# Head and group sums of squares of a mixer block: one fp32 pass over the squares, or two fp32r passes over their high and low part

## The chip, the cores and the metric

The kernel runs on one core of a Trainium2 chip. Its time is the device time of one execution, in microseconds (us). The engines are TensorE (PE in the profile, its weight loads PEld), VectorE (DVE), ScalarE (ACT), GpSimd (POOL) and SyncE (SP), which issues nearly all loads.

## The reference

Two transformer blocks run one after the other on 512 tokens of width 1024. The change is in the mixer of the first one:

```python
    z = u @ w_in
    c0 = 3 * CONV_WIDTH
    cb, cc, ch = jnp.split(z[..., :c0], 3, axis=-1)
    rq, rk, rv, rg = jnp.split(z[..., c0:], 4, axis=-1)
    y_conv = cb * causal_dwconv3(cc * ch, conv_w)
    y_conv = group_rms_norm(y_conv, conv_norm_g, CONV_GROUPS)
    ...
    o = chunkwise_retention(q, k, v).reshape(b, s, RET_WIDTH)
    y_ret = group_rms_norm(o, ret_norm_g, RET_HEADS) * jax.nn.silu(rg)
    return jnp.concatenate([y_conv, y_ret], axis=-1) @ w_out
```

`group_rms_norm` divides each value by the root of the mean square of its group: 128 channels for each of the 4 retention heads, 64 for each of the 8 convolution groups.

## The kernel before

Everything is held with channels on the 128 partitions and the 512 tokens along the row, so a sum over a group of channels is a sum over partitions. TensorE makes it by multiplying the squares with a matrix of ones (`ones`, one head of 128) or with a block matrix (`group64`, two groups of 64).

Every product with a weight is three fp32r matmuls: the weight tile `raw` is split by ScalarE into `w_hi` (L893) and by GpSimd into `w_lo` = raw - w_hi (L443), the activations are split in the same way (`u_hi`, `u_lo`, later `y_hi`, `y_lo`), and a *unit* (L480) adds w_hi·u_hi, w_hi·u_lo and w_lo·u_hi over 8 chunks: 24 matmuls. Weight tiles go through 4 slots. The sums of squares, the retention scores and the transposes are plain fp32 matmuls.

Each engine runs its own list of instructions in the order in which the code is written; semaphores tie the lists together. The stage around the change comes right after the first norm, at about 46 to 232 us.

- **Retention, 4 heads.** A loop pass j of TensorE is `ret(j, j-1)`: unit 0 (v) of head j, the scores of head j-1 (`ret_scores`, L551), unit 1 (q), the output of head j-1 (`ret_out`, L558, which releases the semaphore `ret_o`), the transposes of v, unit 2 (k), then `ret_sum` (L564), and unit 3 (the gate). The sum of head 3 comes in the convolution's opening, behind that stage's first unit 2. The third score matmul of a head waits until VectorE has multiplied the first with its decay (`sdec`, L1384).
- ScalarE copies the head's output (`osb`, L989), squares it (`nsq`, L990), and takes the root of the sum (`ret_root`, L993).
- VectorE turns v into `vf` (`v_in`, L1353), makes `sdec`, rotates q and k (`rotate`, L1371 to L1376), inverts the root (L1389), applies gain and gate, makes `y_lo` (L1400) and the gate of the next head (`silus`, L1412).
- **Convolution, 4 pairs of groups.** A loop pass j of TensorE is units 0 and 1 of pair j, `conv_sum(j-1)` (L615), unit 2 of pair j. The sum of the last pair stands inside the first output units (`two_units(st_out, ...)`). VectorE makes the product (`conv_in`, L1432 and L1436), the three taps and two more multiplications (`conv`, L1443 to L1454, which ends in `ycv_done`), ScalarE squares it (`csq`, L1027), TensorE sums it, ScalarE takes the root (`conv_root`, L1030), VectorE inverts it (L1458) and normalizes.
- ScalarE splits weight tiles between these steps (`ahead`); the first two splits for the output projection stand behind the last `conv_root`.

Of the kernel before, what the change touches and what calls it, by code (L numbers as in the profile page):

```python
# [25 lines left out]
F32R = mybir.dt.float32r  # L26
# [4 lines left out]
P = 128  # L31
T = 512
# [108 lines left out]
def wait(eng, sem, n):  # L141

    if not isinstance(n, int) or n > 0:
        eng.wait_ge(sem, n)
# [23 lines left out]
def build(nc, tab, x, norm1_g, w_in, conv_w, conv_norm_g, ret_norm_g, w_out, norm2_g, w_up, w_down,  # L168
# [23 lines left out]
    with ctx:  # L192
        def sb(name, shape, dt=F32, where=ctx):
            return where.enter_context(nc.sbuf_tensor(name, shape, dt))
# [3 lines left out]
        def sem(name):  # L198
            if name not in sems:
                sems[name] = ctx.enter_context(nc.semaphore(name))  # L200
            return sems[name]
# [32 lines left out]
        start = ExitStack()  # L234
        xtok = sb("xtok", [P, NT, D], where=start)
        start.close()
        acc = sb("acc", [P, 6 * D], where=one)
        mix = ExitStack()
        rope = sb("rope", [P, 2, T], where=mix)
# [226 lines left out]
        def _(pe):  # L466
# [93 lines left out]
                last.then_inc(sem("ret_o"), 1)  # L560

            def ret_sum(p):
                pe.wait_ge(sem("osq_ready"), p + 1)
                pe.matmul(ps[:, SA, :], ones[:], nsq[:, 0, :], start=True, stop=True).then_inc(sem("ret_sum"), 1)  # L564

            def ret(j, p):
                unit(st_ret, 0, j, u_hi, u_lo)
# [43 lines left out]


            def conv_sum(p):
                pe.wait_ge(sem("csq_ready"), p + 1)
                pe.matmul(ps[:, SB, :], group64, nsq[:, 1, :], start=True, stop=True  # L615
                          ).then_inc(sem("conv_sum"), 1)

            unit(st_conv, 0, 0, u_hi, u_lo)
            ret_scores(NQ - 1)
# [265 lines left out]
        def _(act):  # L885
# [101 lines left out]
            def osq(p):  # L987
                act.wait_ge(sem("ret_o"), p + 1)
                act.activation(osb[:], ps[:, OU, :], ACT.Copy).then_inc(sem("osb_ready"), 1)  # L989
                act.activation(nsq[:, 0, :], ps[:, OU, :], ACT.Square).then_inc(sem("osq_ready"), 1)  # L990
            def ret_root(p):
                act.wait_ge(sem("ret_sum"), p + 1)
                act.activation(nrs[:], ps[:, SA, :], ACT.Sqrt, bias=epsc[:, 0:1], scale=1.0 / P  # L993
                               ).then_inc(sem("ret_root"), 1)
# [29 lines left out]
            def csq(j):  # L1024
                act.wait_ge(sem("ycv_done"), j + 1)
                wait(act, sem("conv_sum"), j)
                act.activation(nsq[:, 1, :], ycv[:], ACT.Square).then_inc(sem("csq_ready"), 1)  # L1027
            def conv_root(p):
                act.wait_ge(sem("conv_sum"), p + 1)
                act.activation(sg[:], ps[:, SB, :], ACT.Sqrt, bias=epsc[:, 0:1], scale=1.0 / HD  # L1030
                               ).then_inc(sem("conv_root"), 1)
# [223 lines left out]
        def _(dve):  # L1255
# [110 lines left out]
            def rotate(s, j, dst):  # L1366

                dve.wait_ge(used[s], st_ret.turn(s, j) + 1)
                h = P // 2
                dve.wait_ge(sem("rotated"), 2 * j + s - 1) if not (isinstance(j, int) and 2 * j + s - 1 <= 0) else None  # L1370
                dve.tensor_tensor(nt[0:h, 2, :], ps[h:P, s, :], sinr[h:P, :], ALU.mult).then_inc(sem("swapped"), 1)  # L1371
                dve.tensor_tensor(nt[h:P, 2, :], ps[0:h, s, :], sinr[0:h, :], ALU.mult).then_inc(sem("swapped"), 1)
                dve.tensor_tensor(dst[:], ps[:, s, :], cosr, ALU.mult).then_inc(bank_free[s], 1)
                dve.wait_ge(sem("swapped"), 4 * j + 2 * s)
                dve.wait_ge(bank_free[s], st_ret.turn(s, j) + 1)
                dve.tensor_tensor(dst[:], dst[:], nt[:, 2, :], ALU.add).then_inc(sem("rotated"), 1)  # L1376
                dve.wait_ge(sem("rotated"), 2 * j + s)
                dve.sem_inc(sem("qk_ready"), 1)

            def ret_decay(p):  # L1380
                for b in range(NT):
# [2 lines left out]
                    dve.tensor_tensor(sdec[:, b:b + 1, 0:n], ps[:, SA + b % 2:SA + b % 2 + 1, 0:n],  # L1384
                                      decay[:, ds(p, 1), 0:n], ALU.mult).then_inc(sem("sdec_ready"), 1)

            def ret_norm(p):
                dve.wait_ge(sem("ret_root"), p + 1)
                dve.reciprocal(nrs[:], nrs[:]).then_inc(sem("ret_rinv"), 1)  # L1389
                dve.wait_ge(sem("ret_rinv"), p + 1)  # L1390
                dve.wait_ge(sem("osb_ready"), p + 1)
                dve.scalar_tensor_tensor(nt[:, 0, :], osb[:], vec[:, ds(VAT["ret_norm_g"] + p, 1)], nrs[:],
                                         ALU.mult, ALU.mult).then_inc(sem("ret_t"), 1)
                dve.wait_ge(sem("ret_t"), p + 1)
                dve.wait_ge(sem("silu_ready"), p + 1)
                dve.tensor_tensor(nt[:, 1, :], nt[:, 0, :], silu[:], ALU.mult).then_inc(sem("ret_y"), 1)
# [13 lines left out]
            def silus(j):  # L1410
                dve.wait_ge(sem("sg_ready"), j + 1)
                dve.tensor_tensor(silu[:], silu[:], sg[:], ALU.mult).then_inc(sem("silu_ready"), 1)  # L1412
# [2 lines left out]
            rotate(2, 0, kf)  # L1415
            gate_in(0)
            silus(0)
            with dve.Fori(1, NQ) as j:
                v_in(j)
                ret_decay(j - 1)  # L1420
                rotate(1, j, qf)
                rotate(2, j, kf)
                ret_norm(j - 1)
                gate_in(j)
                ret_lo(j - 1)
                silus(j)


            def conv_in(j):
                dve.wait_ge(used[0], st_conv.turn(0, j) + 1)  # L1430
                wait(dve, sem("prod_ready"), j)
                dve.tensor_tensor(ccs[:], ps[:, 0, :], r1sq[:], ALU.mult).then_inc(bank_free[0], 1)  # L1432
                dve.wait_ge(used[1], st_conv.turn(1, j) + 1)
                dve.wait_ge(bank_free[0], st_conv.turn(0, j) + 1)
                wait(dve, sem("conv_y3"), j)
                dve.tensor_tensor(prod[:, 2:T + 2], ps[:, 1, :], ccs[:], ALU.mult).then_inc(sem("prod_ready"), 1)  # L1436
                dve.wait_ge(sem("prod_ready"), j + 1)
                dve.sem_inc(bank_free[1], 1)
# [26 lines left out]

            ret_decay(NQ - 1)
            dve.wait_ge(sem("vf_turned"), NQ)
            dve.tensor_tensor(r1sq[:], r1[:], r1[:], ALU.mult).then_inc(sem("r1sq"), 1)
            dve.wait_ge(sem("r1sq"), 1)
            conv_in(0)  # L1470
            ret_norm(NQ - 1)
            ret_lo(NQ - 1)
            dve.wait_ge(sem("masks"), 2)
            conv(0)
            with dve.Fori(1, NQ) as j:
                conv_in(j)
                conv_norm(j - 1)
                conv(j)
            conv_norm(NQ - 1)
            dve.wait_ge(sem("ycv_ready"), NQ)  # L1480
            dve.sem_inc(sem("mix_done"), 1)
# [52 lines left out]
            def mlp(st, name, scale, with_ada, next_norm, factor=None):  # L1534
# [63 lines left out]
                for i in range(2):  # L1598
# [1 line left out]

            dve.wait_ge(sem("brow_out"), 16 * NQ)
            dve.tensor_tensor(gsq[:], vec[:, VAT["final_norm_g"]:VAT["final_norm_g"] + KC],
                              vec[:, VAT["final_norm_g"]:VAT["final_norm_g"] + KC], ALU.mult).then_inc(sem("gsq"), 1)
            dve.wait_ge(sem("gsq"), 1)
            dve.tensor_scalar(gones[:], ones[:], gsq[:, KC - 1:KC], None, ALU.mult).then_inc(sem("gones"), 1)
            mlp(st_mlp, "mlp", None, True, "n3", factor=nrs)
            dve.wait_ge(sem("gains"), 2)
# [188 lines left out]
```

## Time and profile before

| | |
|---|---|
| three runs | 1453.22, 1456.02, 1457.69 us, median 1456.02 |
| the profiled execution | 1455.06 us, of which the traced span is 1453.2 us |
| TensorE busy | 1416.0 us, 97% of the span |
| VectorE, ScalarE, GpSimd busy | 794.0, 491.5, 567.8 us |
| mean granted TensorE clock | 0.983 |
| fp32 sums of squares touched by the change | 8, of 2 matmul records each, 0.59 us a record |

An fp32 matmul of 512 columns shows as two records. Records of TensorE overlap, so what one costs is read from the distance between starts and not from its length. The number in brackets at the end of a row is the time in which the engine had nothing to do before it, and who ended that.

### The profile page before, as it was taken

The numbers are of one execution on the slowest core, as the hardware profiler recorded it, in microseconds if no ns is written. First come the engines' busy times: TensorE is split into PE (matmuls) and PEld (weight loads), VectorE is DVE, ScalarE is ACT, GpSimd is POOL, SyncE is SP. The second block draws the span as 40 slices with busy tenths as digits, with TensorE's granted clock in tenths as the row PEclk, the third lists the DMA queues.
The fourth block names the chain that finished last, engine by engine and source line by source line (L and its number), as shares of the span: only waits on it lengthen the run. The fifth ranks groups of instructions, "written<-read, shape, count | busy, mean of one in ns | idle before, by whom it ended". The sixth has DMA issues, their size and how long they took to land.

```text
span 1453.2 us, 18921 instructions
## 1 busy us (share of the span) xinstructions
PE 1416.0 (97%) x6382; PEld 1116.0 (77%) x6382; DVE 794.0 (55%) x1094; ACT 491.5 (34%) x717; POOL 567.8 (39%) x230
## 2 busy tenths in 40 slices
PE   7999999999999999999999999999989999999998
PEld 6677777888787888876667666788868888888886
DVE  6655666485766757876998444311235535253343
ACT  4332324332323223235433333332335323142243
POOL 3433334363454544422212211344343635445441
PEclk9999999999999999979999999999999999999998
DMA  7643234464664746434112121233332423324231
GB/s 200 134 91 91 72 87 145 116 180 124 184 189 133 202 123 180 110 109 139 53 49 57 45 58 44 73 89 103 98 101 72 117 76 113 98 80 121 74 87 58
DMA packets 244644, 155.40 MB, mean 107 GB/s; under 512 B 7764, under 2 KB 237520, under 8 KB 244344
## 3 DMA queue, kind: packets, MB, share of 16 engines
q1 hardware_dynamic: 244136, 153.56, 37.7%
q10 hardware_dynamic: 464, 1.27, 0.3%
q8 instruction: 25, 0.41, 0.1%
q14 instruction: 19, 0.16, 0.0%
HBM read 150.08 MB, written 4.73 MB: 107 GB/s over the span
## 4 chain that ended last, share of the span: by engine, by line
PE 51%; DVE 2%; ACT 1%; issue 0%; DVEq 0%; ACTq 0%
PE ps L480 41%; PE ps L824 3%; PE ps L732 3%; PE ps L758 1%; PE ps L749 1%; PE ps L736 1%; DVE prob L1685 0%; DVE work L1712 0%; PE ps L719 0%; PE ps L543 0%; PE ps L738 0%; DVE top L1710 0%; DVE nt L1648 0%; DVE prob L1677 0%; DVE otok L1772 0%
## 5 line engine op out<-in xcount | busy, mean ns | idle before, releaser
L443 POOL TENSOR_TENSOR w_lo<-raw,w_hi 128x1024 fp32r<-128x1024 f32 x222 | 563.9, 2547 | 853.7 <-ACT w_hi L893 849.9
L480 PE MATMUL ps<-u_hi,w_hi 128*128 128x512 f32 x1080 | 433.9, 402 | 10.0 <-DVE u_lo L1297 3.8
L480 PE MATMUL ps<-u_hi,w_lo 128*128 128x512 f32 x1080 | 423.3, 392 | 0.0
L480 PE MATMUL ps<-u_lo,w_hi 128*128 128x512 f32 x1080 | 423.0, 392 | 0.0
L893 ACT ACTIVATE w_hi<-raw 128x1024 fp32r<-128x1024 f32 x221 | 231.7, 1052 | 201.3 <-PE ps L480 104.2
L480 PEld LDWEIGHTS ps<-u_hi,w_hi 128*128 128x128 f32 x1080 | 204.7, 190 | 61.7 <-issue 14.2
L480 PEld LDWEIGHTS ps<-u_hi,w_lo 128*128 128x128 f32 x1080 | 204.0, 189 | 43.7
L480 PEld LDWEIGHTS ps<-u_lo,w_hi 128*128 128x128 f32 x1080 | 204.6, 189 | 42.6 <-issue 2.2
L480 PE MATMUL ps<-y_hi,w_hi 128*128 128x512 f32 x576 | 225.9, 392 | 1.5 <-POOL w_lo L443 1.4
L480 PE MATMUL ps<-y_hi,w_lo 128*128 128x512 f32 x576 | 224.9, 390 | 0.0
L480 PE MATMUL ps<-y_lo,w_hi 128*128 128x512 f32 x576 | 224.7, 390 | 0.0
L1542 DVE TENSOR_TENSOR nt<-nsq 128x512 f32<-128x512 f32 x64 | 82.1, 1282 | 139.8 <-ACT nsq L1077 137.3
L480 PEld LDWEIGHTS ps<-y_hi,w_hi 128*128 128x128 f32 x576 | 108.5, 188 | 25.0 <-POOL w_lo L443 2.6
L480 PEld LDWEIGHTS ps<-y_lo,w_hi 128*128 128x128 f32 x576 | 108.5, 188 | 22.7 <-issue 0.2
L480 PEld LDWEIGHTS ps<-y_hi,w_lo 128*128 128x128 f32 x576 | 108.4, 188 | 22.7
L1565 DVE TENSOR_TENSOR nt<-ps,nrs 128x512 f32<-128x512 f32 x64 | 44.2, 690 | 141.3 <-PE ps L480 138.0
L1077 ACT ACTIVATE nsq<-ps 128x512 f32<-128x512 f32 x64 | 38.0, 594 | 218.9 <-PE ps L480 218.7
L1547 DVE TENSOR_TENSOR y_lo<-nt,y_hi 128x512 f32 x64 | 95.3, 1489 | 13.2 <-DVE nt L1542 7.0
L1515 DVE SCALAR_TENSOR_TENSOR acc<-adaw,vec,acc 128x1536 f32 (+1 forms) x28 | 76.5, 2733 | 3.6 <-DVE y_lo L1547 3.3
L1165 ACT ACTIVATE prob<-prob,mneg 128x128 f32<-128x128 f32 (+3 forms) x64 | 36.0, 563 | 93.8 <-DVE mneg L1677 93.0
L905 ACT ACTIVATE nsq<-xres 128x512 f32<-128x512 f32 (+1 forms) x40 | 24.9, 627 | 100.6 <-DVE xres L1569 37.6
L1752 DVE TENSOR_TENSOR nt<-ps,nsq 128x512 f32<-128x512 f32 x8 | 5.5, 692 | 92.7 <-PE ps L824 92.7
(211 smaller groups left out, 1250.7 us busy)
## 6 DMA issues: line engine op xcount, KB each, us to landing
raw<-w_in SPq DMA_DIRECT2D x69, 512.0 KB, 3.8
raw<-w_mlp SPq DMA_DIRECT2D x64, 512.0 KB, 3.9
adaw<-w_ada SPq DMA_DIRECT2D x32, 768.0 KB, 4.6
raw<-w_up SPq DMA_DIRECT2D x32, 512.0 KB, 6.3
raw<-w_down SPq DMA_DIRECT2D x32, 512.0 KB, 6.7
raw<-w_out SPq DMA_DIRECT2D x16, 512.0 KB, 3.7
bias_rows<-fbrow SPq DMA_DIRECT2D x4, 640.0 KB
xtok<-x SPq DMA_DIRECT2D x4, 512.0 KB, 6.3
```

The lines of the kernel that those rows point to most:

```text
L443: pool.tensor_tensor(w_lo[:, s, :], raw[:, s, :], w_hi[:, s, :], ALU.subtract).then_inc(lo_ready[s], 1)
L480: last = pe.matmul(ps[0:cols, bank, :], w[:, s, c], r[:, k, :], start=(k == ks[0] and w is w_hi and r is r_hi), stop=(k == ks[-1] and w is ...
L732: pe.matmul(ps[:, bank, 0:keys], qa[b:b + HD, i * P:(i + 1) * P], ka[b:b + HD, 0:keys], start=True, stop=False)
L824: last = pe.matmul(ps[:, b, :], w[:, 2, c], r[:, k, :], start=(k == k0 and w is w_hi and r is y_hi), stop=(k == k0 + NQ - 1 and w is w_lo))
L893: act.activation(w_hi[:, t, :], raw[:, t, :], ACT.Copy).then_inc(hi_ready[t], 1)
L905: act.activation(nsq[:, n % 2:n % 2 + 1, :], xres[:, ds(m, 1), :], ACT.Square).then_inc(sem("norm_sq"), 1)
L1077: act.activation(nsq[:, s % 2, :], ps[:, s, :], ACT.Relu).then_inc(bank_free[s], 1)
L1165: act.activation(prob[:, n % 2, 0:keys], prob[:, n % 2, 0:keys], ACT.Exp, bias=mneg[:, n:n + 1], scale=-1.0, accum_out=rowsum[:, n:n + 1]) ...
L1515: dve.scalar_tensor_tensor(a, adaw[:, b, :], c, a, ALU.mult, ALU.add).then_inc(sem("acc_done"), 1)
L1542: dve.tensor_tensor(nt[:, s % 2, :], nsq[:, s % 2, :], nsq[:, s % 2, :], ALU.mult).then_inc(sem("mlp_sq"), 1)
L1547: dve.tensor_tensor(y_lo[:, m, :], nt[:, s % 2:s % 2 + 1, :], y_hi[:, m, :], ALU.subtract).then_inc(sem("mlp_h"), 1)
L1565: dve.tensor_tensor(nt[:, 0, :], ps[:, s, :], factor[:], ALU.mult).then_inc(bank_free[s], 1)
```

## The change

The squares are made twice on ScalarE: as before in fp32 (`nsq`), and once more rounded to fp32r (`sq_hi`). VectorE subtracts the two (`sq_lo`, new functions `osq_low` and `csq_low`). The sum is two fp32r matmuls, over `sq_hi` and over `sq_lo`, in place of one fp32 matmul. The two summing matrices are copied once to fp32r, ahead of VectorE's retention loop. The new tiles lie where `acc` and the rows of x lie at other times. The semaphores `r1sq` and `gsq` become one (`squares`).

```diff
@@ tensor
             def ret_sum(p):
-                pe.wait_ge(sem("osq_ready"), p + 1)
-                pe.matmul(ps[:, SA, :], ones[:], nsq[:, 0, :], start=True, stop=True).then_inc(sem("ret_sum"), 1)
+                pe.wait_ge(sem("masks"), 5)
+                pe.wait_ge(sem("squares_low"), p + 1)
+                pe.matmul(ps[:, SA, :], ones_r[:], sq_hi[:], start=True, stop=False)
+                pe.matmul(ps[:, SA, :], ones_r[:], sq_lo[:], start=False, stop=True).then_inc(sem("ret_sum"), 1)
...
             def conv_sum(p):
-                pe.wait_ge(sem("csq_ready"), p + 1)
-                pe.matmul(ps[:, SB, :], group64, nsq[:, 1, :], start=True, stop=True
-                          ).then_inc(sem("conv_sum"), 1)
+                pe.wait_ge(sem("squares_low"), NQ + p + 1)
+                pe.matmul(ps[:, SB, :], group_r[:], sq_hi[:], start=True, stop=False)
+                pe.matmul(ps[:, SB, :], group_r[:], sq_lo[:], start=False, stop=True).then_inc(sem("conv_sum"), 1)
@@ scalar
             def osq(p):
                 act.wait_ge(sem("ret_o"), p + 1)
                 act.activation(osb[:], ps[:, OU, :], ACT.Copy).then_inc(sem("osb_ready"), 1)
+                wait(act, sem("ret_sum"), p)
                 act.activation(nsq[:, 0, :], ps[:, OU, :], ACT.Square).then_inc(sem("osq_ready"), 1)
+                act.activation(sq_hi[:], ps[:, OU, :], ACT.Square).then_inc(sem("osq_ready"), 1)
...
                 act.activation(nsq[:, 1, :], ycv[:], ACT.Square).then_inc(sem("csq_ready"), 1)
+                act.activation(sq_hi[:], ycv[:], ACT.Square).then_inc(sem("csq_ready"), 1)
@@ vector
+            def osq_low(p):
+                dve.wait_ge(sem("osq_ready"), 2 * p + 2)
+                dve.tensor_tensor(sq_lo[:], nsq[:, 0, :], sq_hi[:], ALU.subtract).then_inc(sem("squares_low"), 1)
+
+            def csq_low(p):
+                dve.wait_ge(sem("csq_ready"), 2 * p + 2)
+                dve.tensor_tensor(sq_lo[:], nsq[:, 1, :], sq_hi[:], ALU.subtract).then_inc(sem("squares_low"), 1)
...
             silus(0)
+            dve.wait_ge(sem("const"), 2)
+            dve.tensor_copy(ones_r[:], ones[:]).then_inc(sem("masks"), 1)
+            dve.tensor_copy(group_r[:], group64).then_inc(sem("masks"), 1)
             with dve.Fori(1, NQ) as j:
                 v_in(j)
                 ret_decay(j - 1)
                 rotate(1, j, qf)
+                osq_low(j - 1)
                 rotate(2, j, kf)
...
+            osq_low(NQ - 1)
             conv_in(0)
...
             with dve.Fori(1, NQ) as j:
+                csq_low(j - 1)
                 conv_in(j)
                 conv_norm(j - 1)
                 conv(j)
+            csq_low(NQ - 1)
             conv_norm(NQ - 1)
```

On VectorE, just ahead of and at the start of the retention loop (L1412 is `silus`, L1353 `v_in`), the kernel before has:

```order
L1412 TENSOR_TENSOR silu<-silu,sg 128x512 [waits bank_free3,sg_ready]
L1418 UNCONDITIONAL_BRANCH
L1418 ISA
L1353 TENSOR_TENSOR vf<-ps,r 128x512 [waits vf_turned,used0]
L1382 ISA [waits bank_free0]
L1384 ISA [waits ret_s]
```

and the changed one:

```order
L1430 TENSOR_TENSOR silu<-silu,sg 128x512 [waits bank_free3,sg_ready]
L1437 CAST ones_r<-ones 128x128 [waits const]
L1438 CAST group_r<-small 128x128
L1439 UNCONDITIONAL_BRANCH
L1439 ISA
L1363 TENSOR_TENSOR vf<-ps,r 128x512 [waits vf_turned,used0]
```

Two casts stand between the first head's gate and the second head's v.

On VectorE, at the head of the convolution's loop pass (the two multiplications of `conv_in`, then the reciprocal of `conv_norm`), the kernel before has:

```order
L1454 TENSOR_TENSOR ycv<-ycv,r 128x512 [waits bank_free2]
L1475 UNCONDITIONAL_BRANCH
L1475 ISA
L1432 TENSOR_TENSOR vf<-ps,qf 128x512 [waits prod_ready,used0]
L1436 TENSOR_TENSOR prod<-ps,vf 128x512 [waits conv_y3,bank_free0,used1]
```

and the changed one:

```order
L1476 TENSOR_TENSOR ycv<-ycv,r 128x512 [waits bank_free2]
L1498 UNCONDITIONAL_BRANCH
L1498 ISA
L1403 TENSOR_TENSOR sq_lo<-nsq,sq_hi 128x512 [waits csq_ready]
L1452 REGISTER_ALU
L1454 TENSOR_TENSOR vf<-ps,qf 128x512 [waits prod_ready,used0]
L1458 TENSOR_TENSOR prod<-ps,vf 128x512 [waits conv_y3,bank_free0,used1]
```

The subtraction stands ahead of `conv_in`, and waits for both squares of the pair before.

On TensorE, in the same loop pass between unit 1 and unit 2, the kernel before has:

```order
L480 MATMUL ps<-u_hi,w_lo 128x512
L615 MATMUL ps<-nsq,small 128x512 [waits csq_ready]
L480 MATMUL ps<-u_hi,w_hi 128x512 [waits bank_free2,lo_ready2]
L480 MATMUL ps<-u_lo,w_hi 128x512
L480 MATMUL ps<-u_hi,w_lo 128x512
```

and the changed one:

```order
L485 MATMUL ps<-u_hi,w_lo 128x512
L621 REGISTER_ALU
L622 MATMUL ps<-sq_hi,group_r 128x512 [waits squares_low]
L623 MATMUL ps<-sq_lo,group_r 128x512
L485 MATMUL ps<-u_hi,w_hi 128x512 [waits bank_free2,lo_ready2]
```

Both new matmuls stand behind the wait for VectorE's subtraction, and no matmul has changed its place around them.

## Rows read from the trace of the kernel before

**Rows 1.** The page, part 1: busy time, share of the span, instructions.

```profile
PE 1416.0 (97%) x6382; PEld 1116.0 (77%) x6382; DVE 794.0 (55%) x1094; ACT 491.5 (34%) x717; POOL 567.8 (39%) x230
```

**Rows 2.** Waits, 40 to 225 us: who waited for whom, us, times, longest.

```profile
PE ps L551 <- DVE sdec L1384: 1.4, 3, 0.7
```

**Rows 3.** TensorE's timeline at a retention sum: start, us, line, operation.

```profile
67.04 0.39 PE L480 MATMUL ps<-u_hi,w_lo 128*128 128x512 f32 x1
67.27 1.02 PE L564 MATMUL ps<-nsq,ones 128*128 128x512 f32 x2
...
68.36 0.40 PE L480 MATMUL ps<-u_lo,w_hi 128*128 128x512 f32 x1
```

**Rows 4.** ScalarE's timeline in the same pass.

```profile
62.03 0.59 ACT L990 ACTIVATE nsq<-ps 128x512 f32<-128x512 f32 x1
```

**Rows 5.** VectorE's timeline at the end of that pass.

```profile
78.34 0.69 DVE L1412 TENSOR_TENSOR silu<-silu,sg 128x512 f32<-128x512 f32 x1
79.25 0.69 DVE L1353 TENSOR_TENSOR vf<-ps,r 128x512 f32<-128x512 f32 x1 [0.23 <-PE ps L480]
```

**Rows 6.** TensorE's timeline at the first convolution sum.

```profile
162.60 0.39 PE L480 MATMUL ps<-u_hi,w_lo 128*128 128x512 f32 x1
165.36 2.08 PE L615 MATMUL ps<-nsq,small 128*128 128x512 f32 x2 [2.38 <-ACT nsq L1027]
...
168.86 0.39 PE L480 MATMUL ps<-u_lo,w_hi 128*128 128x512 f32 x1
```

**Rows 7.** ScalarE's timeline, convolution stage.

```profile
164.68 0.63 ACT L1027 ACTIVATE nsq<-ycv 128x512 f32<-128x512 f32 x1 [5.37 <-DVE ycv L1454]
165.21 1.04 ACT L893 ACTIVATE w_hi<-raw 128x1024 fp32r<-128x1024 f32 x1
...
197.60 0.63 ACT L1027 ACTIVATE nsq<-ycv 128x512 f32<-128x512 f32 x1 [5.56 <-DVE ycv L1454]
...
212.85 0.63 ACT L1027 ACTIVATE nsq<-ycv 128x512 f32<-128x512 f32 x1 [4.54 <-DVE ycv L1454]
...
215.28 2.00 ACT L893 ACTIVATE w_hi<-raw 128x1024 fp32r<-128x1024 f32 x2
```

**Rows 8.** TensorE's timeline from the third convolution sum into the output projection.

```profile
201.53 1.02 PE L615 MATMUL ps<-nsq,small 128*128 128x512 f32 x2
...
213.08 0.39 PE L480 MATMUL ps<-y_hi,w_lo 128*128 128x512 f32 x1
213.53 1.12 PE L615 MATMUL ps<-nsq,small 128*128 128x512 f32 x2
...
218.87 0.50 PE L480 MATMUL ps<-y_hi,w_hi 128*128 128x512 f32 x1
...
232.81 0.50 PE L480 MATMUL ps<-y_hi,w_hi 128*128 128x512 f32 x1 [1.41 <-POOL w_lo L443]
```

**Rows 9.** VectorE's timeline: the reciprocals behind two of the sums.

```profile
152.82 3.35 DVE L1389 RECIPROCAL nrs<-nrs 128x512 f32<-128x512 f32 x1 [8.50 <-ACT nrs L993]
...
168.19 3.35 DVE L1458 RECIPROCAL sg<-sg 128x512 f32<-128x512 f32 x1 [2.25 <-ACT sg L1030]
```

**Rows 10.** VectorE's timeline: two copies of 128x128, and the second head's v.

```profile
21.07 0.22 DVE L1342 CAST causalb<-small 128x128 bf16<-128x128 f32 x1
...
51.14 0.68 DVE L1353 TENSOR_TENSOR vf<-ps,r 128x512 f32<-128x512 f32 x1
...
649.25 2.40 DVE L1622 COPY sel<-causalb 128x128 bf16<-128x128 bf16 x1
```

**Rows 11.** GpSimd's timeline at the same two places.

```profile
51.52 4.71 POOL L443 TENSOR_TENSOR w_lo<-raw,w_hi 128x1024 fp32r<-128x1024 f32 x2 [9.65 <-ACT w_hi L893]
...
648.99 4.96 POOL L443 TENSOR_TENSOR w_lo<-raw,w_hi 128x1024 fp32r<-128x1024 f32 x2 [6.00 <-ACT w_hi L893]
```

**Rows 12.** Windows of 1 and 3 us: stretch, its length, busy us of each engine, granted clock, DMA.

```profile
166.00:167.00 1.00, 1.00 (x3) 0.34 (x1) 0.00 (x0) 0.25 (x1) 0.67 (x1) 0.50 0.00 0
...
231.00:234.00 3.00, 1.59 (x7) 1.01 (x6) 2.38 (x2) 2.05 (x3) 2.63 (x2) 1.00 0.00 0
```

More of the change, by code:

```diff
@@ L236, in build @@
         start.close()
+        sums = ExitStack()
+        sb("fbrow_room", [P, NREL], where=sums)
+        sq_hi, sq_lo = sb("sq_hi", [P, T], F32R, where=sums), sb("sq_lo", [P, T], F32R, where=sums)
+        ones_r, group_r = sb("ones_r", [P, P], F32R, where=sums), sb("group_r", [P, P], F32R, where=sums)
+        sums.close()
         acc = sb("acc", [P, 6 * D], where=one)
@@ L1467, in _ @@
             dve.wait_ge(sem("vf_turned"), NQ)
-            dve.tensor_tensor(r1sq[:], r1[:], r1[:], ALU.mult).then_inc(sem("r1sq"), 1)
-            dve.wait_ge(sem("r1sq"), 1)
+            dve.tensor_tensor(r1sq[:], r1[:], r1[:], ALU.mult).then_inc(sem("squares"), 1)
+            dve.wait_ge(sem("squares"), 1)
+            osq_low(NQ - 1)
             conv_in(0)
@@ L1602, in _ @@
             dve.tensor_tensor(gsq[:], vec[:, VAT["final_norm_g"]:VAT["final_norm_g"] + KC],
-                              vec[:, VAT["final_norm_g"]:VAT["final_norm_g"] + KC], ALU.mult).then_inc(sem("gsq"), 1)
-            dve.wait_ge(sem("gsq"), 1)
+                              vec[:, VAT["final_norm_g"]:VAT["final_norm_g"] + KC], ALU.mult).then_inc(sem("squares"), 1)
+            dve.wait_ge(sem("squares"), 2)
             dve.tensor_scalar(gones[:], ones[:], gsq[:, KC - 1:KC], None, ALU.mult).then_inc(sem("gones"), 1)
```

## The prediction

> **What bounds the kernel now.** I read the page first: TensorE is busy for 1416.0 us, 97% of the span [rows 1]. So an edit counts by what it does to TensorE's row of work: matmul time taken out of it is gained, and time in which it stands still is lost. Then I read the timelines of TensorE, ScalarE, VectorE and GpSimd around the eight sums, to see at each sum whether TensorE arrives after the squares (a spare squaring then costs nothing) or before them (then all that is added to the squares' way is paid).
>
> In the retention loop TensorE comes late to every sum. In the pass shown the squares start at 62.03 and take 0.59 us [rows 4], and the sum starts at 67.27 with no idle time before it, 0.23 us after the matmul in front [rows 3]. In the convolution it differs from sum to sum. At the first one TensorE has started its last matmul at 162.60, stands still for 2.38 us, and starts at 165.36, 0.05 us after the square has ended (164.68 + 0.63 = 165.31) [rows 6, 7]. At the third the square ends at 198.23 and TensorE arrives at 201.53, so 3.3 us are spare [rows 7, 8]; the second stands in the same place of its pass, and TensorE doesn't wait there either. At the fourth TensorE could start at 213.08 + 0.23 = 213.31, and starts at 213.53, right behind the square's end at 213.48 [rows 7, 8]. So two of the eight sums, the first and the last of the convolution, hang on the squares.
>
> **What a sum costs on TensorE.** The sum starts at 67.27 and the second matmul behind it at 68.36; take off one matmul of 0.23, and the fp32 sum holds TensorE for 1.09 - 0.23 = 0.86 us [rows 3]. Two fp32r matmuls of the same 512 columns take 2 x 0.23 = 0.46, so each sum gives back 0.40 us. I take the row's spacing also for a weight matrix of ones: the weights' values do not show in any spacing.
>
> **The retention sums.** The added Square (0.59 alone, 0.5 in a row of them) and the subtraction (a VectorE operation of this shape takes 0.69 [rows 5]) end at about 62.6 + 0.5 + 0.8 = 63.9, and the sum starts at 67.27: 3.4 us of cover, in which VectorE has nothing to do either until unit 2 is done. Without that cover each would cost 1.3 us, as below. The saving of 0.40 is not all kept. In passes 1 and 2 the next thing TensorE waits for is `sdec` of the next head [rows 2], and in front of that stands `v_in`, which VectorE can't start before it is through with `silus`: that starts at 78.34 and ends at 79.03, and the next operation can begin a little ahead of that end, so at about 78.95, against 79.25 before [rows 5]. `silus` hangs on unit 2 and the rotation of k, which are ahead of the sum, so it doesn't move. These two passes give 0.30 us each. The third pass is followed by the convolution, with no `v_in`, and the fourth sum's way goes through the root to a VectorE that waited 8.50 us for it [rows 9]: 0.40 each. Together -1.40 us; the bounds are -1.2 and -1.6.
>
> **The two copies.** They stand between `silus(0)` and `v_in(1)`, which began without idle time at 51.14 [rows 10]. The cast of 128x128 took 0.22 us [rows 10]; two, laid a little into each other as all these operations are, move `v_in` by 0.3 to 0.44. In this pass TensorE waits for `sdec` already (0.7 us is the longest of the three waits [rows 2]), so it is paid: +0.35.
>
> **The convolution sums.** Behind the first square now come the second (the next operation of ScalarE starts 0.53 us after it [rows 7]), a hand-over to VectorE, taken as the 0.05 of rows 6 and 7, and the subtraction of 0.69 with a hand-over in place of the old one. The sum starts 0.53 + 0.05 + 0.69 = 1.27, taken as 1.3 us later (bounds 1.2 and 1.45). `conv_in(1)` is queued behind that subtraction; it takes 1.4 us, and VectorE had 2.25 us to spare before the reciprocal [rows 9], so it stays hidden. In the passes of the second and third sum `conv_in` is late by 1.2 us too, but there its second multiplication waits for unit 1 of TensorE anyway. These two sums cost nothing and give 0.40 each. The fourth: +1.3, and ScalarE's root, the two weight splits behind it at 215.28, GpSimd's `w_lo` and so TensorE's next unit at 218.87, which waits for that, all move with it [rows 7, 8]. They move by 1.3 - 0.40, since the sum itself is shorter. The first sum works the same way, and its 0.40 comes off TensorE's row too. In all: 2 x 1.3 - 4 x 0.40 = +1.00.
>
> Every one of these moves what comes after: the DVE chain of the next pass and TensorE's row are tied at sums 1 and 4, and between them TensorE runs without a gap.
>
> **The sum.** -1.40 + 0.35 + 1.00 = -0.05 us: a wash. The profiled execution took 1455.06 us (span 1453.2, 1.9 around it) and would take 1455.0. It lies 0.96 below the median of the runs, 1456.02, so the median would be 1456.0. TensorE would be less busy by 8 x 0.40 = 3.2 us, and stand still for as much more. What this kernel's measurement can tell from no change is about 0.3%, or 4.4 us.
>
> **Rivals.**
> *The copies run into GpSimd.* A copy of 128x128 from SBUF to SBUF took 2.40 us at 649.25, where GpSimd had begun two `w_lo` at 648.99: it ended when the first of them was through (648.99 + 2.4), against 0.22 where GpSimd was quiet [rows 10, 11]. The new copies would start at 51.14 and about 51.3; GpSimd begins two `w_lo` at 51.52 [rows 11]. If the second copy is late by more than 0.2 us, it waits until 51.5 + 2.4 = 53.9, `v_in` starts at 54.1 in place of 51.5, and TensorE loses 2.6 us more: 1458.6. If the first is late by 0.4 as well, each waits for one of the two `w_lo`, until 56.3: +4.9 us, 1460.9, which is slower by 0.33%. That is the mechanism on the other side, and the point from which it decides is 0.4 us of delay at one place. The Trainium skill (SBUF — State Buffer, section "Who interferes with whom") says that copies and casts within SBUF can hold the port pair shared with GpSimd, that whoever issues first keeps it for the whole instruction and that the other blocks. The trace agrees [rows 10, 11], and by that rule the order of issue alone decides. Against the rival: nothing ahead of the copies is changed, and that distance comes out of fixed times.
>
> *TensorE's clock drops at the fourth convolution sum.* At the first sum, behind 2.38 us of standing still, the granted clock was 0.50 [rows 12], that is 1.2 instead of 2.4 GHz, and it took 3.50 us from the sum's start to the second `u_lo` matmul after it [rows 6]. At the higher clock that would be 1.09 + 3 x 0.23 = 1.78 us [rows 3], so 1.72 us were lost. With the change TensorE waits about 1.5 us at the fourth sum. Behind the wait of 1.41 us before 232.81 the clock stayed at 1.00 [rows 8, 12]. 1.5 is nearer to that one, so I leave it out; otherwise +1.7: 1457.7. At the first sum the wait grows from 2.4 to 3.7, where the clock drops anyway; it may stay down a little longer or shorter, 0.9 us either way.
>
> *The low part is hidden.* If the chain in front of the first and last sum were not lengthened on TensorE's side, because something else is later there, the kernel would win up to 3.2 - 0.35: 1453.1. Against it: in both places TensorE starts within 0.05 us of the square.
>
> **How the numbers follow.** The wash 0.68; one copy blocked 0.12; both blocked, or one with the clock's drop, 0.06; the clock's drop alone 0.10; the hidden low part 0.04. The case of 0.06 lies at or just above +4.4 us and is the chance of slower; the gain of the last case stays short of -4.4, and faster gets 0.03 for the spread of the runs (1453.22 to 1457.69). The rest, 0.91, is no change. The range runs from 1453.8 (0.8 us below the wash by the bounds of the retention part, the copies and the two waits, and 1.4 for the spread of a median) to 1459.0 (one copy blocked, 1458.6, and the upper bounds).
>
> **What the profile after would show.** Right: eight pairs of fp32r matmuls 0.23 apart; the second squares 0.5 us behind the first; TensorE idle about 3.7 us before the first and 1.5 us before the fourth convolution sum, for VectorE's subtraction; no idle time before the other six; the sum at 213.5 moved by under half a microsecond; both copies under 0.3 us. Wrong: a copy of 2.4 us; a clock of 0.50 behind the fourth sum; a wait before a retention sum; or matmuls on `ones_r` further apart than 0.23.

## The result, and the profile after

| | before | changed |
|---|---|---|
| median of 8 runs each | 1454.93 us (1451.26 to 1457.69) | 1460.85 us (1458.77 to 1461.86) |
| the profiled execution | 1455.06 us, span 1453.2 | 1459.32 us, span 1457.4 |
| mean granted TensorE clock | 0.983 | 0.987 |

The ratio of changed to before is 1.0037; the brackets behind a ratio give its 95% interval, here [1.0026, 1.0049]. (The ratio is not exactly that of the medians.) So the changed kernel is slower, by 5.9 us of the medians and by 5.4 of the ratio. I had forecast no change, 1456.0, with 1459.0 as the upper end.

The page of the changed kernel, part 1:

```profile
PE 1409.0 (97%) x6378; PEld 1114.3 (76%) x6382; DVE 807.4 (55%) x1104; ACT 495.3 (34%) x725; POOL 567.7 (39%) x230
```

TensorE is busy for 7.0 us less than before [rows 1] and the span is 4.2 us longer, so by the records TensorE stands still for 11 us more. (Of the 7.0, 4.4 lie between the two blocks, from 615 to 683 us before, where the granted clock was 0.85 and is now 0.92. The stage around the sums has only 0.4 of them: there the sums are shorter and the clock is lower, 0.96 against 0.98.) Where is in the chain of waits. The changed kernel, TensorE's waits from 40 to 235 us (total, times, longest, in us):

```profile
PE ps L556 <- DVE sdec L1394: 9.3, 4, 2.6
PE ps L622 <- DVE sq_lo L1403: 5.0, 2, 3.6
```

The second row is the price that I had forecast: two convolution sums that wait, for 3.7 and 1.5 us by the forecast. The first row was 1.4 us before [rows 2] and should have grown by the copies' share alone. (Some 1.6 us of its growth are the clock's, in the first pass; they come back further down.) So I went to VectorE, between `rotate` of k and the next `sdec`. The changed kernel, VectorE:

```profile
70.10 0.69 DVE L1383 TENSOR_TENSOR kf<-ps,rope 128x512 f32<-128x512 f32 x1
70.89 2.90 DVE L1386 TENSOR_TENSOR kf<-kf,nt 128x512 f32<-128x512 f32 x1
73.93 3.35 DVE L1407 RECIPROCAL nrs<-nrs 128x512 f32<-128x512 f32 x1
...
82.34 0.69 DVE L1363 TENSOR_TENSOR vf<-ps,r 128x512 f32<-128x512 f32 x1
```

and GpSimd in the same stretch:

```profile
65.81 2.39 POOL L448 TENSOR_TENSOR w_lo<-raw,w_hi 128x1024 fp32r<-128x1024 f32 x1 [10.28 <-ACT w_hi L900]
70.84 2.40 POOL L448 TENSOR_TENSOR w_lo<-raw,w_hi 128x1024 fp32r<-128x1024 f32 x1 [2.65 <-ACT w_hi L900]
```

The last addition into `kf`, which reads two tiles of SBUF, takes 2.90 us, and did nothing else than before. In the trace of the kernel before the same two operations read as follows:

```profile
69.70 0.69 DVE L1376 TENSOR_TENSOR kf<-kf,nt 128x512 f32<-128x512 f32 x1
```

```profile
70.03 2.62 POOL L443 TENSOR_TENSOR w_lo<-raw,w_hi 128x1024 fp32r<-128x1024 f32 x1 [3.50 <-ACT w_hi L893]
```

Before, the addition was first by 0.33 us, and took 0.69. After, `w_lo` is first by 0.05 us (70.84 against 70.89), and the addition ends at 73.79, half a microsecond behind the end of `w_lo` at 73.24. What moved `w_lo` is ScalarE. Before:

```profile
68.32 0.69 ACT L993 ACTIVATE nrs<-ps,epsc 128x512 f32<-128x512 f32 x1 [2.96 <-PE ps L564]
68.91 1.05 ACT L893 ACTIVATE w_hi<-raw 128x1024 fp32r<-128x1024 f32 x1
```

After:

```profile
69.13 0.69 ACT L1002 ACTIVATE nrs<-ps,epsc 128x512 f32<-128x512 f32 x1 [2.10 <-PE ps L571]
69.71 1.05 ACT L900 ACTIVATE w_hi<-raw 128x1024 fp32r<-128x1024 f32 x1
```

The root waits for the sum, the fourth split of the pass is queued behind the root, and `w_lo` waits for that split. VectorE's rotation starts from unit 2, ahead of the sum, and the shorter sum doesn't move it. From the first step of the rotation (67.46 before, 68.66 after) the root now comes 0.47 us behind in place of 0.86: it is 0.39 us nearer, the whole saving of the sum, and the addition had only 0.33 us in hand. The slower addition is the meeting of these two operations, called the port lock below.

The same happens in all three passes of the loop (2.90, 2.89, 2.90 us). VectorE's chain comes late by 2.2 us, and TensorE waits for it at the third score matmul of the head. TensorE in the changed kernel, at the two sums' matmuls, then at the three score matmuls:

```profile
68.46 0.40 PE L570 MATMUL ps<-sq_hi,ones_r 128*128 128x512 f32 x1
68.69 0.40 PE L571 MATMUL ps<-sq_lo,ones_r 128*128 128x512 f32 x1
...
84.13 1.62 PE L556 MATMUL ps<-qf,kf 128*128 128x256 f32 x4 [2.63 <-DVE sdec L1394]
...
115.76 0.95 PE L556 MATMUL ps<-qf,kf 128*128 128x256 f32 x4 [2.64 <-DVE sdec L1394]
...
144.75 0.95 PE L556 MATMUL ps<-qf,kf 128*128 128x256 f32 x4 [1.60 <-DVE sdec L1394]
...
173.79 0.79 PE L622 MATMUL ps<-sq_hi,group_r 128*128 128x512 f32 x1 [3.64 <-DVE sq_lo L1403]
...
223.16 0.50 PE L622 MATMUL ps<-sq_hi,group_r 128*128 128x512 f32 x1 [1.33 <-DVE sq_lo L1403]
```

From the first retention sum to the start of the fourth head's output, TensorE needs 82.55 us (68.46 to 151.01) in place of 76.16 (67.27 to 143.43). These 6.39 us are, within 0.02, 6.04 of longer waits (the three grew by 2.32, 2.31 and 1.41 us) and 1.59 of half the clock behind the first of them, less 3 x 0.42 of shorter sums. The Trainium skill (SBUF — State Buffer, section "Who interferes with whom") counts a VectorE operation with two SBUF inputs among those that contend with GpSimd for the shared port pair. The trace agrees: 2.90 against 0.69 us.

### The profile page after: what moved, and what is told of

Read it like the earlier page. It is cut to its first block, busy times and chain, and to the rows that moved or that the text cites. A ratio compares the mean times of both kernels' runs of the same rounds, so it can differ in the third digit from the quotient of the medians.

```text
span 1457.4 us, 18951 instructions
## 1 busy us (share of the span) xinstructions
PE 1409.0 (97%) x6378; PEld 1114.3 (76%) x6382; DVE 807.4 (55%) x1104; ACT 495.3 (34%) x725; POOL 567.7 (39%) x230
## 3 DMA queue, kind: packets, MB, share of 16 engines
q10 hardware_dynamic: 464, 1.27, 0.3%
## 4 chain that ended last, share of the span: by engine, by line
PE 79%; DVE 12%; issue 4%; ACT 2%; POOL 2%; DMA 1%; DVEq 0%; ACTq 0%; POOLq 0%
PE ps L485 67%; PE ps L831 3%; PE ps L739 3%; POOL w_lo L448 2%; PE ps L765 1%; DVE acc L1540 1%; PE ps L756 1%; DVE nrs L1407 1%; DVE xres L1594 1%; DVE kf L1386 1%; DVE xres L1641 1%; PE ps L563 1%; PE ps L743 0%; ACT nsq L912 0%; ACT w_hi L900 0%
```

## The experiments

The kernel before was timed anew beside each group of experiments, on the same chip as they: 1456.07 us beside the first four, 1455.15 beside the next four, 1455.24 beside the last. "The retention part" is the stretch just named; before it lasts 76.16 us, and 76.18 and 76.16 in two more executions of the kernel before. "The addition" is `kf<-kf,nt` in the loop. In the texts written ahead of each experiment, theory 1 is the port lock; theory 2 is the rival named there; "rival 3" is the thought that the longer waits of the convolution are what costs, and not the third rival of the prediction. "The stage" in them is longer than the retention part, and a paragraph at the end of this section has it for all kernels.

**A longer sum again.** Each retention sum's pair is issued twice, so TensorE does more than in the changed kernel and everything else is the same.

```diff
                 pe.matmul(ps[:, SA, :], ones_r[:], sq_hi[:], start=True, stop=False)
+                pe.matmul(ps[:, SA, :], ones_r[:], sq_lo[:], start=False, stop=True)
+                pe.matmul(ps[:, SA, :], ones_r[:], sq_hi[:], start=True, stop=False)
                 pe.matmul(ps[:, SA, :], ones_r[:], sq_lo[:], start=False, stop=True).then_inc(sem("ret_sum"), 1)
```

> The changed kernel with each retention sum issued twice (four fp32r passes, the second pair overwrites the first), so that TensorE holds the sum for about 0.92 us again, against 0.86 before and 0.46 in the changed kernel. Theory 1 (port lock: the shorter sum lets GpSimd's w_lo start ahead of VectorE's last add into kf): more TensorE work makes the kernel faster. The add into kf takes 0.69 us again instead of 2.90 in all three passes, and the stage from the first score matmul to the second row of output units, 183.8 us before and 193.7 in the changed kernel, is 185 to 187. Ratio to before about 1.001 to 1.002. Theory 2 (the second Square and the subtraction ahead of the rotation of k make the loop late): as the changed kernel or up to 1.8 us slower, 1.004 to 1.005, add into kf still 2.9.

Median 1454.94 us, before 1456.07; ratio 0.9997 [0.9988, 1.0007], a little under the 1.001 to 1.002 that I expected. The retention part is 76.37 us. VectorE's addition and GpSimd's `w_lo` in this kernel:

```profile
72.67 0.69 DVE L1388 TENSOR_TENSOR kf<-kf,nt 128x512 f32<-128x512 f32 x1
```

```profile
73.08 2.53 POOL L448 TENSOR_TENSOR w_lo<-raw,w_hi 128x1024 fp32r<-128x1024 f32 x1 [3.10 <-ACT w_hi L902]
```

With eight more matmuls than the changed kernel it is as fast as before, and some 6 us faster than the changed one: the addition is ahead again, by 0.41 us. Both squares, the subtraction, the copies and all convolution sums are still there, so none of them costs these 6 us by itself.

**The split ahead of the root.** ScalarE makes the fourth split before it waits for the sum.

```diff
                 ahead(st_ret, 2, j)
-                ret_root(p)
                 ahead(st_ret, 3, j)
+                ret_root(p)
                 sigmoid(j)
```

> The changed kernel, with ScalarE's fourth weight split of a retention pass put ahead of the root instead of behind it, so that GpSimd makes both w_lo before k is rotated. Theory 1: add into kf 0.69, v_in of the next head about 0.3 us earlier than before relative to unit 2; stage 183.5 to 186, ratio 0.999 to 1.001. Theory 2: no change against the changed kernel, 1.004.

Median 1454.64 us; ratio 0.9993 [0.9981, 1.0005]; retention part 75.13 us. GpSimd makes both `w_lo` in one go. It is through at 70.67, 0.31 us before VectorE begins the addition, which runs undisturbed:

```profile
65.90 4.77 POOL L448 TENSOR_TENSOR w_lo<-raw,w_hi 128x1024 fp32r<-128x1024 f32 x2 [10.29 <-ACT w_hi L900]
```

```profile
70.98 0.69 DVE L1386 TENSOR_TENSOR kf<-kf,nt 128x512 f32<-128x512 f32 x1
```

Here the shorter sums are kept (75.13 is 1.03 under before), and the whole change comes to the wash that I had forecast for it.

**The halves of the change.** One kernel keeps the new convolution sums alone, one the new retention sums alone.

```diff
@@ convolution alone: the retention's sum as before, with its second square, osq_low and ones_r gone
+                pe.wait_ge(sem("osq_ready"), p + 1)
+                pe.matmul(ps[:, SA, :], ones[:], nsq[:, 0, :], start=True, stop=True).then_inc(sem("ret_sum"), 1)
@@ retention alone: the convolution's sum as before, with its second square, csq_low and group_r gone
+                pe.wait_ge(sem("csq_ready"), p + 1)
+                pe.matmul(ps[:, SB, :], group64, nsq[:, 1, :], start=True, stop=True
+                          ).then_inc(sem("conv_sum"), 1)
```

> Only the convolution sums changed, the retention sums in fp32 as before. Theory 1: the first and the last convolution sum 1.3 us later behind the square, four sums 0.4 shorter: stage 184.8 to 186 (the upper end if the low clock lasts longer behind the first wait), ratio 1.0007 to 1.0015. If the convolution's longer waits are what costs (rival 3), ratio 1.003 or more.

Median 1455.14 us; 0.9996 [0.9987, 1.0005]; retention part 76.16, waits of 3.71 and 1.42 us before the first and the fourth convolution sum. The waits came as expected. The time didn't show them: 1.0007 was the lower end of what I expected, and the interval ends at 1.0005. One or two microseconds are less than this kernel's executions scatter by (last section), so the price of the convolution half is read from the trace alone.

> Only the retention sums changed, the convolution sums in fp32 as before. Theory 1: add into kf 2.9 us in three passes; VectorE's delay of 2.2 costs TensorE about 2.3, 2.3 and 1.4 at the scores, less 4 x 0.4, plus 0.3 for the copy, plus 0 to 3.4 where the clock falls behind these waits: stage 188 to 192, ratio 1.003 to 1.005. If the convolution is what costs (rival 3): 1.000.

Median 1459.05 us; 1.0027 [1.0015, 1.0038], at the lower end of what I expected; retention part 82.53 us. The slowdown is in this half. VectorE and GpSimd in it:

```profile
72.24 2.90 DVE L1385 TENSOR_TENSOR kf<-kf,nt 128x512 f32<-128x512 f32 x1
```

```profile
72.19 2.40 POOL L448 TENSOR_TENSOR w_lo<-raw,w_hi 128x1024 fp32r<-128x1024 f32 x1 [2.63 <-ACT w_hi L900]
```

**Two and three passes in the kernel before.** This takes the collision away from everything else that the change does. Nothing is added on VectorE's loop or on ScalarE; the one square is written rounded, the low part is left out, and the loop's range is 2 in one kernel and 3 in the other. One pass takes 0.23 us. In both, `ones` is copied to `ones_r` ahead of the first norm's reciprocal, where VectorE waits anyway.

```diff
+                pe.wait_ge(sem("masks"), 4)
                 pe.wait_ge(sem("osq_ready"), p + 1)
-                pe.matmul(ps[:, SA, :], ones[:], nsq[:, 0, :], start=True, stop=True).then_inc(sem("ret_sum"), 1)
+                for _ in range(2):
+                    last = pe.matmul(ps[:, SA, :], ones_r[:], sq_hi[:], start=True, stop=True)
+                last.then_inc(sem("ret_sum"), 1)
...
-                act.activation(nsq[:, 0, :], ps[:, OU, :], ACT.Square).then_inc(sem("osq_ready"), 1)
+                act.activation(sq_hi[:], ps[:, OU, :], ACT.Square).then_inc(sem("osq_ready"), 1)
```

> The kernel before with each retention sum as two fp32r passes over the rounded squares, the second overwriting the first, so the low part is left out of the sum; one square per head, no subtraction, no copy in the way. The sum holds TensorE for 0.46 us as in the changed kernel, but nothing is added on ScalarE or VectorE. Theory 1: the shorter sum alone brings the collision: add into kf 2.9 us in three passes, stage 188 to 191, ratio 1.002 to 1.004. Theory 2: 1.6 us faster than before, stage 182.2, ratio 0.999.

Median 1461.18 us, before 1455.15; 1.0038 [1.0023, 1.0053]; retention part 82.29 us.

```profile
70.18 2.89 DVE L1385 TENSOR_TENSOR kf<-kf,nt 128x512 f32<-128x512 f32 x1
```

```profile
70.12 2.40 POOL L447 TENSOR_TENSOR w_lo<-raw,w_hi 128x1024 fp32r<-128x1024 f32 x1 [3.12 <-ACT w_hi L900]
```

> The same with three passes, 0.69 us a sum, 0.17 shorter than before. GpSimd's w_lo started 0.33 us behind the add into kf before, so by theory 1 it starts 0.16 behind it now and there is no collision: add 0.69 us, stage 183.1 to 183.6, ratio 0.999 to 1.0005, and so faster than the kernel with two passes although it does one pass more. Theory 2: between the two-pass kernel and before, in proportion.

Median 1452.63 us; 0.9990 [0.9977, 1.0002]; retention part 75.69 us.

```profile
70.25 0.69 DVE L1385 TENSOR_TENSOR kf<-kf,nt 128x512 f32<-128x512 f32 x1
```

```profile
70.43 2.77 POOL L447 TENSOR_TENSOR w_lo<-raw,w_hi 128x1024 fp32r<-128x1024 f32 x1 [3.36 <-ACT w_hi L900]
```

The edit that, but for that copy, only shortens the sum costs as much as the whole change. One matmul more in each sum puts `w_lo` 0.18 us behind the addition's start (I had expected 0.16), and the kernel is 8.5 us faster by the medians, 7.0 by the two ratios and 6.6 by the retention part.

**Was it the order of split and root in itself?** The swap of the second experiment, in the kernel before.

> The kernel before with the fourth weight split ahead of the root and nothing else, as the control of the two kernels with that swap. Theory 1: there is no collision to take away, so stage 183.8 and ratio 1.000 (0.999 to 1.001). If the swap is a gain of its own: 0.998.

Median 1455.82 us; 1.0006 [0.9994, 1.0018]; retention part 76.16, the addition 0.69 us. The swap alone gives nothing. It pays only where the shorter sum is there.

**The part that pays, without the part that costs.** The retention half alone, the split ahead of the root, and the copy of `ones` ahead of the first norm's reciprocal, where VectorE waits anyway.

```diff
                 ahead(st_ret, 2, j)
-                ret_root(p)
                 ahead(st_ret, 3, j)
+                ret_root(p)
...
                 add_square("n1", m)
+            dve.wait_ge(sem("const"), 2)
+            dve.tensor_copy(ones_r[:], ones[:]).then_inc(sem("masks"), 1)
             dve.wait_ge(sem("norm_root"), 1)
```

> Only the retention sums in two passes, ScalarE's fourth weight split of a pass ahead of the root, and the copy of the ones moved to VectorE's wait for the first norm. Theory 1: the add into kf 0.69 us, the four retention sums give their 0.3, 0.3, 0.4 and 0.4, the convolution is as before: stage from the first score matmul to the second row of output units 182.3 us against 183.8 before, ratio 0.9985 to 1.0. Theory 2 (the added square and subtraction cost time in the retention loop): stage above 184.

Median 1451.66 us; 0.9975 [0.9966, 0.9984]: faster than both kernels, and by more than the 0.9985 that was the lower end of what I expected. The retention part is 75.16 us, 1.00 under before, which is 0.30 + 0.30 + 0.40 as forecast for the three sums in it. The fourth sum gives 0.40 more. Another 0.42 us come from a place that I hadn't looked at: with the copy where it now is, the first head's addition into `kf` starts 0.80 us behind the operation in front of it in place of 1.21, and the first score matmul comes 14.27 us after the start of the first norm's reciprocal in place of 14.69. The kernels with two and three passes, which have the same copy there, show the same; no other kernel does, and why is not shown. That makes 1.8 of the measured 3.5 us; where the rest comes from stays open.

Does the added square and subtraction cost time in the loop, as theory 2 says? The whole stage took 184.38 us, above the 184 that stood for it. But 1.97 us of that lie ahead of the first retention sum, where two more executions of the unchanged kernel took as long; from the first retention sum on it is 164.19 us against 165.54 before, 1.35 less, which is the four sums. So the added work shows no cost there.

**The convolution's two waits, without the subtraction.** The retention sums are as before. In the convolution both squares are made, the sum takes the high one alone, and the low part is left out.

```diff
-                pe.wait_ge(sem("squares_low"), NQ + p + 1)
-                pe.matmul(ps[:, SB, :], group_r[:], sq_hi[:], start=True, stop=False)
-                pe.matmul(ps[:, SB, :], group_r[:], sq_lo[:], start=False, stop=True).then_inc(sem("conv_sum"), 1)
+                pe.wait_ge(sem("masks"), 4)
+                pe.wait_ge(sem("csq_ready"), 2 * p + 2)
+                pe.matmul(ps[:, SB, :], group_r[:], sq_hi[:], start=True, stop=True).then_inc(sem("conv_sum"), 1)
```

> Only the convolution sums changed, and of them only the pass over the high part, with both squares made but neither a subtraction nor a low pass, so the low part is left out of the sum. By the terms of the prediction the wait of TensorE at the first sum falls from the 3.7 us of the kernel with both parts to 2.38 + 0.55 = 2.9, and at the fourth from 1.4 to 0.8; the sum is 0.23 long. If the subtraction is not what makes up the rest of the 1.3 us, the waits stay at 3.7 and 1.4.

Median 1455.41 us, before 1455.24; 1.0009 [0.9989, 1.0028]. TensorE in this kernel, at the first and the fourth sum:

```profile
167.62 0.50 PE L621 MATMUL ps<-sq_hi,group_r 128*128 128x512 f32 x1 [2.90 <-ACT sq_hi L1033]
...
214.50 0.47 PE L621 MATMUL ps<-sq_hi,group_r 128*128 128x512 f32 x1 [0.70 <-ACT sq_hi L1033]
```

Waits of 2.90 and 0.70 us, where 2.9 and 0.8 were expected. Against 2.38 before [rows 6], 0.5 of the first wait is the second square, and the rest up to 3.64 to 3.71, some 0.8, is the subtraction with its hand-over.

**Both kernels once more**, to see what one profile can differ by.

> The kernel before, profiled once more, for the part behind the changed stage. Its first profile spent 67.1 us between the first summing matmul of the norm between the two blocks and the first attention score, with the clock at 0.50 from 619 to 639 us, where the changed kernel and most of its variants spent 62.3 to 64.5. Theory A (chance of the clock in one execution): 62 to 65 in one of the two repeats. Theory B (the kernel's own): 67 in both. The retention part, from the first sum to the fourth head's output, 76.2 us in either.

> As the one before: a second repeat of the kernel before. Theory A: anything from 62 to 67 us; theory B: 67.

> The changed kernel, profiled once more. The add into kf 2.9 us in all three passes again, retention part 80.9 us plus what the clock takes (82.55 in the first profile), whole stage 190 to 194; the part between the blocks anything from 62 to 67 us by theory A, 63 by theory B.

The kernel before took 1452.42 and 1457.82 us, the changed one 1463.5. The addition took 2.90 us in all three passes of the changed one again, and its retention part 82.56 us. Between the blocks the kernel before took 62.7 and 67.0 us, so theory A holds (last section), and the changed one 62.4.

**The whole stage**, from the first score matmul to the second row of output units, in us:

| kernel | expected | measured | of it ahead of the first retention sum |
|---|---|---|---|
| before, three executions | | 183.76, 184.00, 185.35 | 18.22, 20.06, 19.85 |
| changed, two executions | second: 190 to 194 | 193.67, 193.79 | 20.09, 20.11 |
| pair issued twice | 185 to 187 | 185.18 | 20.11 |
| split ahead | 183.5 to 186 | 185.07 | 20.11 |
| convolution alone | 184.8 to 186 | 186.36 | 19.84 |
| retention alone | 188 to 192 | 191.51 | 19.97 |
| two passes | 188 to 191 | 187.87 | 18.22 |
| three passes | 183.1 to 183.6 | 181.51 | 18.23 |
| before, split ahead | 183.8 | 182.15 | 18.24 |
| retention alone, split ahead | 182.3 | 184.38 | 20.19 |

Five of the nine miss, two of them by under 0.4 us. The others are off by the 1.6 to 2 us that the clock gives or takes at two places. Ahead of the first retention sum the unchanged kernel itself took 18.2 us or about 20. And from the first to the second convolution sum, behind the same wait of 2.4 us, it took 18.94 and 18.91 us in two executions and 17.33 in the third; the kernels with two passes, with three, and the kernel before with the split ahead took 17.31. The retention part, which had a loss of clock only in the kernels with the long waits, is the steadier measure.

## Why the prediction was wrong

**The step that failed** is in the part on the retention sums: "`silus` hangs on unit 2 and the rotation of k, which are ahead of the sum, so it doesn't move." By the data that is so. But `silus` is queued behind the last step of the rotation, and how long that step takes depends on GpSimd, whose `w_lo` hangs on ScalarE's split, and that on the root behind the sum. I followed what the shorter sum releases on TensorE and on VectorE. I didn't follow what it releases on ScalarE and GpSimd. I had put the cost of this at nothing. In its place came 2.32 + 2.31 + 1.41 = 6.04 us of waits. The experiments with two and three passes, with the pair issued twice and with the split ahead show that this is the cause, each from another side.

**The rival on the other side** had the right mechanism in the wrong place. I gave the shared port to the two new copies, at +4.9 us and 1460.9. They took 0.22 us each, and `w_lo` began 0.24 us behind the start of the second. That its 1460.9 is next to the measured 1460.85 is chance. (The copy at 649.25 that it rests on ended at 651.65, 0.26 us behind the end of `w_lo`, and not with it.) What I said against it, that nothing ahead of them is changed, was right for the copies. I never asked the same question of the operations that were there already.

**The terms of the sum**, read from the profile after:

| term | forecast | trace |
|---|---|---|
| a retention sum shorter, on TensorE | 0.40 | 0.39 right behind it, 0.42 to the next sum |
| two copies, first score matmul to third | +0.35 | +0.27 |
| first convolution sum later | +1.3 | +1.27 |
| fourth convolution sum later | +1.3 | 0.85 + 0.42 = +1.27 |
| second and third convolution sum | -0.40 each | -0.42 each |
| the wait before the first and the fourth | 3.7 and 1.5 | 3.64 and 1.33 |
| clock behind the fourth sum | 1.00 | 1.00 |
| port lock in the three passes | none | +6.04 |
| clock lost behind the longer waits (first retention wait, first convolution sum) | none, and up to 0.9 either way | +1.6 and +1.2 |

The last but one row is the one that isn't in my sum. The last is partly a consequence of it: behind the 2.63 us of standing still at the second head's scores TensorE ran at 0.50 of its clock, that is 1.2 GHz. (The first window below shows 0.55; from 84.20 to 85.80 alone it is 0.50.) The changed kernel, windows from 84 to 86, 174 to 178 and 224 to 229 us (length, busy us of PE, PEld, DVE, ACT, POOL, granted clock, DMA share, GB/s):

```profile
84.00:86.00 2.00, 1.87 (x6) 1.60 (x7) 1.17 (x4) 0.00 (x0) 2.00 (x2) 0.55 0.02 6
...
174.00:178.00 4.00, 4.00 (x10) 3.13 (x11) 3.26 (x3) 1.63 (x2) 3.62 (x2) 0.50 0.03 8
224.00:229.00 5.00, 4.91 (x22) 3.74 (x21) 4.31 (x2) 2.51 (x3) 3.35 (x2) 1.00 0.02 3
```

The clock doesn't follow from the wait alone, and here the prediction was wrong in a second place: it said that behind a wait of 2.4 us or more at the first convolution sum "the clock drops anyway". In the kernel before, behind the same 2.38 us, the granted clock was 0.56 from 165 to 168 us in one execution and 1.00 from 167 to 170, behind 2.37 us, in another. Behind the other two long waits, at 115.76 and 144.75, the third score matmuls took 0.95 us as before, and in the second execution of the changed kernel they took 1.51 us behind the first wait in place of 1.62.

**The measured rise against the pieces.** In the profiled executions the copies +0.27, the lock +6.04, the two chains in the convolution 2 x 1.27, and eight sums at -0.42 make 0.27 + 6.04 + 2.54 - 3.36 = +5.5 us. With the two losses of clock in the table it is 8.3. The whole stage grew by 9.9 us (183.76 to 193.67), and the last 1.6 are a third loss of clock, behind the first head's third score matmul. The window from 53 to 57 us, first in the kernel before:

```profile
53.00:57.00 4.00, 4.00 (x19) 3.27 (x20) 0.96 (x3) 0.00 (x0) 3.23 (x2) 1.00 0.46 136
```

then in the changed one:

```profile
53.00:57.00 4.00, 4.00 (x14) 3.17 (x13) 0.62 (x2) 0.00 (x0) 2.52 (x2) 0.57 0.46 136
```

This loss is no piece of the change. The first execution of the kernel before ran at half the clock a little earlier, in the first two score matmuls, where TensorE waits for VectorE right after (0.72 us, against 2.11 in another execution at the full clock), so it lost nothing by it; its two other executions needed 20 us to the first retention sum, as the changed kernel does. Behind the stage the kernel before lost what the changed one didn't: 67.1 against 63.1 us between the blocks. So the two traced spans are only 4.2 us apart.

The measured +5.9 us has an interval of 3.8 to 7.1 us. It holds the sum without the clock, and neither the 8.3 nor the 9.9. The profile has the clock of a single execution, and the median has that of many.

## What to carry to other kernels

A piece that gets shorter releases its successors earlier on every engine, so follow each of them to its end, GpSimd's operations too, and compare where they then start with VectorE's operations that read two SBUF tiles. A distance of a third of a microsecond there is a finding, and an edit of 0.4 us can turn it over and cost 2.2 us a pass. Where the work that collides does not depend on what was shortened, move it ahead of the wait, as the split here: that took the loss away and kept the gain. Look at the new distance too: here `w_lo` ends 0.31 us before the addition starts.

## What the runs showed of the hardware

**The first to start wins, by 0.05 us.** With `w_lo` ahead by 0.05 to 0.06 us the addition took 2.89 to 2.90 us in every pass (changed kernel, retention alone, two passes). With the addition ahead by 0.18, 0.33 and 0.41 us it took 0.69, and GpSimd's record grew instead, to 2.77, 2.62 and 2.53 us from 2.40: it grows by 0.37, 0.22 and 0.13 us, a little less than the 0.51, 0.36 and 0.28 that the addition still had to run. So the same meeting costs VectorE 2.2 us or GpSimd 0.1 to 0.4 us. No run has a distance between these.

**One kernel, 4 us apart, by a wait and the clock.** In the kernel before, from the second summing matmul of the second block's norm (L493, counted from its weight load) to the first attention score, one execution took 62.7 us (617.2 to 679.9) and another 67.0 (618.3 to 685.3), with the same instructions. The windows from 617 to 651 us, first of the one execution:

```profile
617.00:651.00 34.00, 30.71 (x141) 24.41 (x140) 30.57 (x35) 13.79 (x20) 7.91 (x3) 0.90 0.43 126
```

then of the other:

```profile
617.00:651.00 34.00, 30.44 (x111) 24.30 (x110) 28.77 (x35) 9.41 (x14) 4.32 (x2) 0.70 0.37 108
```

TensorE is busy for the same 30.4 to 30.7 us, and gets 111 records done in place of 141, at a granted clock of 0.70 in place of 0.90. Of the 4.3 us, 1.6 are a longer wait: TensorE stood still for 1.96 us before the norm's third summing matmul in the one execution and for 3.56 in the other, and behind the longer one the clock was 0.50 from 625 to 640 us. A difference of 4 us is larger than every term of my sum, and the likely reason why the convolution half's microsecond could not be seen in the times.
